# A hybrid decoder step on one core: who issues the cache pages, and a new table of places for the background work

## What is computed

```python
def mla_sample_attention(q_nope, q_rope, c_kv, k_rope, lat_past, kr_past, w_uk, w_uv):
    q_lat = jnp.einsum('bthd,chd->bthc', q_nope, w_uk)
    s_past = (jnp.einsum('bthc,bkc->bhtk', q_lat, lat_past)
              + jnp.einsum('bthr,bkr->bhtk', q_rope, kr_past)).astype(jnp.float32) * scale
    ...
    p = jax.nn.softmax(jnp.concatenate([s_past, s_new], axis=-1), axis=-1).astype(c_kv.dtype)
    o_lat = (jnp.einsum('bhtk,bkc->bthc', p[..., :P], lat_past) + ...)

# lat_past, kr_past: cache_kv_latent[l][page_table], cache_k_rope[l][page_table]:
# 8 sequences x 16 pages of 128 rows, 256 and 32 floats wide

merged = (g0 * (pool_y @ w_pool_out) + g1 * (mla_o @ w_mla_out) + g2 * (mem_o @ w_x_out)) @ w_o
h = x + merged

def peer_ffn(h):            # on rmsnorm(h), for each of 544 tokens
    q = jnp.einsum('nd,dhc->nhc', hf, lp['w_peer_q'])          # "queries"
    s1, s2 = q[..., :128] @ k1.T, q[..., 128:] @ k2.T           # 8 heads
    # top 16 of each, top 16 of their 256 sums: 128 experts a token, of 16384
    a = gelu(einsum('cd,ckd->ck', hc, peer_u[ic]))              # rows u
    return einsum('ck,ckd->cd', gate * a, peer_v[ic])           # rows v
```

## Time and profile before

| | |
|---|---|
| median of 3 runs | 2424.64 us (2421.26 to 2428.17) |
| the profiled execution | 2408.34 us |
| its span, first to last instruction | 2406.4 us |
| busy: PE, DVE, POOL, ACT | 1354.6, 1135.9, 1034.5, 299.8 us |
| moved by DMA | 688.00 MB, 570.49 MB of it by POOL's gathers |
| first gather, first GELU, second GELU | 533.8 us, 878.7 us, 1397.3 us |

### The profile page before, as it was taken

How to read it: one execution, slowest core, us unless ns; L and a number is a source line. 1 busy time by engine, 2 the same in 40 slices (tenths; PEclk the granted TensorE clock), 3 DMA queues, 4 the chain that set the end, 5 groups by cost and what they waited for, 6 DMA issues and landing times.

```text
span 2406.4 us, 22075 instructions
## 1 busy us (share of the span) xinstructions
PE 1354.6 (56%) x7122; PEld 811.6 (34%) x7122; DVE 1135.9 (47%) x2797; ACT 299.8 (12%) x758; POOL 1034.5 (43%) x1098
## 2 busy tenths in 40 slices
PE   7998999995444537898763865510035510035513
PEld 5874788783223324555541621100001100001100
DVE  2104521136757733344598156068967068850060
ACT  2214520022222121001010110000000000000000
POOL 0000000004233524565466146666666676666674
PEclk9998999996677658999876876655567655567656
DMA  6212035548697869999999669999999999999997
GB/s 198 74 59 59 1 105 152 149 128 307 224 309 245 325 249 325 373 374 350 364 386 399 215 235 354 374 391 376 374 352 357 364 391 382 371 353 366 376 382 270
DMA packets 337097, 688.00 MB, mean 286 GB/s; under 512 B 45319, under 2 KB 189608, under 8 KB 336975
## 3 DMA queue, kind: packets, MB, share of 16 engines
q0 software_dynamic: 156672, 570.49, 62.6%
q1 hardware_dynamic: 180311, 116.10, 16.6%
HBM read 682.36 MB, written 4.18 MB: 285 GB/s over the span
## 4 chain that ended last, share of the span: by engine, by line
PE 30%; DVE 22%; issue 12%; DMA 10%; another core or an unknown queue 9%; SPq 7%; POOL 5%; DVEq 3%; ACT 2%; POOLq 0%; ACTq 0%
PE bank L663 23%; DVE arena L1850 15%; POOL arena L629 5%; DMA arena<-in_w_x_out_dram 4%; DVEq L1786 3%; PE bank L659 2%; PE bank L1142 2%; SPq L510 2%; DMA arena<-in_cache_mem_v_dram 2%; SPq L507 2%; DMA arena<-in_peer_v_dram,arena 2%; SPq L504 2%; DMA arena<-in_w_mla_out_dram 1%; SPq L539 1%
## 5 line engine op out<-in xcount | busy, mean ns | idle before, releaser
L629 POOL DMA_INDIRECT arena<-in_peer_u_dram,arena x544 | 512.3, 942 | 926.1 <-DVE arena L1834 531.8
L663 PE MATMUL bank<-arena 128*128 128x256 f32 (+7 forms) x2940 | 714.9, 400 | 93.0 <-issue 48.1
L629 POOL DMA_INDIRECT arena<-in_peer_v_dram,arena x544 | 517.3, 951 | 426.7 <-PE bank L1142 193.0
L1850 DVE CUSTOM_DVE_ANT_0 arena<-arena,bank 128x1024 f32<-128x1024 f32 x544 | 638.1, 1216 | 43.8 <-issue 38.9
L663 PEld LDWEIGHTS bank<-arena 128*128 128x128 f32 (+2 forms) x2940 | 545.4, 194 | 263.2 <-issue 99.8
L1142 PE MATMUL bank<-arena 128*32 128x512 f32 x2176 | 377.8, 829 | 319.7 <-DMA arena<-in_peer_v_dram,arena 239.9
L659 PE MATMUL bank<-arena 128*128 128x128 f32 (+5 forms) x774 | 152.8, 349 | 586.4 <-issue 203.2
L659 PEld LDWEIGHTS bank<-arena 128*128 128x128 f32 (+5 forms) x774 | 117.2, 179 | 634.6 <-issue 246.5
L1142 PEld LDWEIGHTS bank<-arena 128*32 128x32 f32 x2176 | 80.7, 133 | 592.9 <-issue 591.5
L1178 ACT ACTIVATE arena<-bank 128x256 f32<-128x256 f32 (+12 forms) x399 | 156.6, 428 | 510.9 <-PE bank L663 150.4
L1879 DVE TENSOR_TENSOR arena<-arena,bank 128x1024 f32<-128x1024 f32 x5 | 6.1, 1220 | 361.6 <-PE bank L1142 194.3
(11 more groups left out here) (140 smaller groups left out, 722.3 us busy)
## 6 DMA issues: line engine op xcount, KB each, us to landing
arena<-in_w_in_dram SPq DMA_DIRECT2D x48, 512.0 KB
arena<-in_w_peer_q_dram SPq DMA_DIRECT2D x32, 512.0 KB
arena<-in_cache_kv_latent_dram SPq DMA_DIRECT2D x128, 128.0 KB
arena<-in_peer_u_dram,arena POOLq DMA_INDIRECT x544
arena<-in_peer_v_dram,arena POOLq DMA_INDIRECT x544
arena<-in_w_o_dram SPq DMA_DIRECT2D x8, 1024.0 KB, 7.8
arena<-in_w_in_dram SPq DMA_DIRECT2D x6, 1024.0 KB
arena<-in_w_pool_out_dram SPq DMA_DIRECT2D x16, 256.0 KB
```

Source lines behind the costliest of these rows:

```text
L629: pool.indirect_dma_start(out=ring[s % RING], out_offset=None, in_=table[0], in_offset=IndirectOffsetOnAxis(ap=ix, axis=0)).then_inc(land[ ...
L663: last = pe.matmul(dst, lhs(k), rhs(k), start=(k == 0), stop=(k == n - 1))
L1850: dve.tensor_tensor_reduce(ring[s % RING], ring[s % RING], h_dot, 1.0, 0.0, ALU.mult, ALU.add, act_a[:, p % 2, k:k + 1]).then_inc(u_free, 1)
```

## The change

It does two things. ACT gets three of the eight pages of each step from the third step on: `own_pages(s)` names the pages of SP (five) and of ACT (three, each with a table read of its own). ACT issues those of step s + 2 at the end of its third unit of step s. And the numbers in `background_ticks` are new.

```diff
+def own_pages(s):
+
+    mine = [(j, k) for j in range(4) for k in range(PGRP)]
+    return (mine, []) if s < 2 else (mine[0:5], mine[5:])
+
 def background_ticks():
 
     u0, u1 = PLACE["u", 0, 0], PLACE["u", 1, 0]
-    ticks = [u0 + 3 + 23 * i // 12 for i in range(3 * (STEPS + 1))]
...
-    ticks += [u0 + 109 + 7 * i // 4 for i in range(2 * (NB + 2))]
-    ticks += [u0 + 147 + 27 * h // 10 for h in range(2 * MERGE)]
...
-    ticks += [u1 + 74 + 3 * j for j in range(QJ + 2)]
+    ticks = [u0 + 3 + 5 * i // 3 for i in range(3 * (STEPS + 1))]
...
+    ticks += [u0 + 96 + 2 * i for i in range(2 * (NB + 2))]
+    ticks += [u0 + 138 + 13 * h // 5 for h in range(2 * MERGE)]
...
+    ticks += [u1 + 52 + 3 * j for j in range(QJ + 2)]
     return ticks
@@ load_pages on SP
                 for j in range(4):
                     n = (4 * a + j) * PAGES + g * PGRP
-                    _, pages = nc.values_load_multi_w_load_instructions(pagetab[0:1, n:n + PGRP], engines=[mybir.EngineType.SP], min_val=0,
-                                           max_val=cache_lat.shape[1] - 1)
-                    for k, page in enumerate(pages):
+                    ks = [k for jj, k in own_pages(s)[0] if jj == j]
+                    if not ks:
+                        continue
+                    _, pages = nc.values_load_multi_w_load_instructions(
+                        pagetab[0:1, n:n + len(ks)], engines=[mybir.EngineType.SP], min_val=0,
+                        max_val=cache_lat.shape[1] - 1)
+                    for k, page in zip(ks, pages):
@@ on ACT
+            def load_pages(s):
+
+                i, a, g = s % 3, s // HALVES, s % HALVES
+                if s >= 3:
+                    act.wait_ge(pv_mm, s - 2)
+                for j, k in own_pages(s)[1]:
+                    n = (4 * a + j) * PAGES + g * PGRP + k
+                    page = act.value_load(pagetab[0:1, n:n + 1], min_val=0, max_val=cache_lat.shape[1] - 1)
+                    act.dma_start(lat[i][:, j, k],
+                                  cache_lat[0][DynSlice(page, 1)].rearrange("a p c -> (a p) c")).then_inc(
+                        ld_page[i], 16)
+                    act.dma_start(rop[i][:, k, ROPE * j:ROPE * (j + 1)],
+                                  cache_kr[0][DynSlice(page, 1)].rearrange("a p c -> (a p) c")).then_inc(
+                        ld_page[i], 16)
@@ sample on ACT: ahead of the first step, and at the end of a step's third unit
+                act.wait_ge(ld_gain, 16 * 13)
...
+                    if s + 2 < STEPS:
+                        load_pages(s + 2)
```

More of the change, by code:

```diff
@@ L112 @@
 STEPS = 2 * HALVES
+def own_pages(s):
+    mine = [(j, k) for j in range(4) for k in range(PGRP)]
+    return (mine, []) if s < 2 else (mine[0:5], mine[5:])
 def background_ticks():
     u0, u1 = PLACE["u", 0, 0], PLACE["u", 1, 0]
-    ticks = [u0 + 3 + 23 * i // 12 for i in range(3 * (STEPS + 1))]
-    ticks += [u0 + 102 + 2 * i for i in range(3)]
-    ticks += [u0 + 109 + 7 * i // 4 for i in range(2 * (NB + 2))]
-    ticks += [u0 + 147 + 27 * h // 10 for h in range(2 * MERGE)]
-    ticks += [u1 + 22 + 27 * r // 10 for r in range(12)]
-    ticks += [u1 + 56 + 2 * t for t in range(3)]
-    ticks += [u1 + 64 + 3 * t for t in range(3)]
-    ticks += [u1 + 74 + 3 * j for j in range(QJ + 2)]
+    ticks = [u0 + 3 + 5 * i // 3 for i in range(3 * (STEPS + 1))]
+    ticks += [u0 + 90 + 2 * i for i in range(3)]
+    ticks += [u0 + 96 + 2 * i for i in range(2 * (NB + 2))]
+    ticks += [u0 + 138 + 13 * h // 5 for h in range(2 * MERGE)]
+    ticks += [u1 + 11 + 2 * r for r in range(12)]
+    ticks += [u1 + 37 + 2 * t for t in range(3)]
+    ticks += [u1 + 44 + 5 * t // 2 for t in range(3)]
+    ticks += [u1 + 52 + 3 * j for j in range(QJ + 2)]
     return ticks
```

## The result

The change takes 2411.05 us (median of 5 runs, 2405.87 to 2412.52), the kernel before in the same comparison 2426.28 us (2421.26 to 2432.35). The ratio is 0.9932, with an interval of 0.9912 to 0.9953: faster by some 16 us. Run once more beside others (`e11_change_again`) it is 0.9944 [0.9923, 0.9965]. The forecast was "about no change", 2426 us; the time lies in its range, but the change helps, which the forecast gave a chance of 0.35.

A forecast was written before the change was run, and what follows sets the result against it. Length is set by rows and background bytes passing before tile 1's GELU; only DMA rest can be won. Terms -10 + 3 + 12.5 - 4 = +1.5 us on 2424.64 gave 2426 us, range 2402 to 2450.

The forecast's parts named there:

- 13 steps, 13.1 to 12.3 us: Steps without DVE's picking: three pages on ACT shorten each from 13.1 to 12.3 us, -10 us (-30 to +13).
- two pick intervals: Two steps with DVE's picking of experts: ACT's 5.4 us of pages come on top, half shows, +3 us (0 to +11).
- rows fewer at the merge's start: New ticks: 9 rows fewer through when the merge begins, if the background takes the same time, 1.39 us each, +12.5 us.
- memory rounds and the way to the merge: Rounds of 11.5 us have room for four rows; later GELU of tile 0 mostly hidden by the ring: 0, up to +8.
- behind it: queries, stop: Queries start 31 us earlier, 1.2 of them cross POOL's stop ahead of tile 1's GELU, 3.2 us each: -4 us.
- The cost of a page: ACT's issue of one page, two DMAs and a table read: 1.56 to 2.07 us, three taken as 5.4 us.
- The rival that counted their window in full: Queries ahead of tile 1's GELU: 6 move at 4.85 us each, -20 instead of -4, 2410 us; chance 0.17.
- The slower rival: Steps: ACT's six DMAs each wait out one of SP's, 14.3 us a step, +27 in all, 2452 us; slower had chance 0.29.
- The carried 16 us: Whole kernel: the median's 16 us over the profiled 2408.34 us, carried over to the forecast, gathers taken to cost the same.

The follow-up runs named there:

- e11_change_again: The change once more, nothing altered, run beside other kernels: 0.9944 of the kernel before.
- e2_ticks_only: The change with all eight pages of every step on SP, only the ticks new: 0.9969 of the kernel before, 7.5 us less.
- e6_memory_13_later: The change with every tick behind the 16 steps 13 rows later, two rows to a memory unit: 0.9984 of the kernel before, 2422 us.
- e1_pages_only: The change with the ticks of before, so only the three pages on ACT are new: 0.9943 of the kernel before, 14 us less.
- e9_sparse: Two thirds of the queries behind the GELU of tile 1, seven rows to a step, six to a memory round, against the change: 0.9862 of before.
- e12_sparse_all_on_sp: The change with late queries, seven rows to a step and six to a memory round, and all pages back on SP: 0.9871 of the kernel before.
- e3_queries_back: The change with the queries' ticks 22 rows later, as before the change: 0.9917 of the kernel before.
- e7: The change with memory rounds from tick 90, all 20 memory units ahead of the GELU of tile 0, merge from 127: 0.9907 of before, 2404 us.
- e5_before_again: The kernel before once more, nothing changed, for a second profile: ratio 1.0012, profiled execution 2404.95 us.
- e4_queries_late: The change with twelve of the 18 query units put behind the GELU of tile 1: 0.9743 of the kernel before, 62 us less.

## Why the prediction was wrong

Between two chips of equal speed (the profiles of before and of `e11_change_again`) the sum reads, forecast and measured:

| term | forecast | measured |
|---|---|---|
| 13 steps, 13.1 to 12.3 us | -10 | 12.2 us: -11.8 |
| two pick intervals | +3 | -1.8 |
| rows fewer at the merge's start | 9 rows, +12.5 | 12 rows, +16.7 |
| memory rounds and the way to the merge | 0 | -9.9 |
| behind it: queries, stop | -4 | -1.5 |
| sum | +1.5 | -7.7 (with 0.6 for the first step's later start) |

**The step that failed** is the third term with its condition, "If the background took the same time". The rows were fewer, and each was paid for in the full stretch as the step says, but the background did not take the same time: the same 57 rows passed in 124.4 us instead of 134.3 (6.4 to 9.9 us less, over the two profiles of each kernel). The text took the rounds' 11.5 us as the rounds' own and saw room in them; it did not ask what POOL waited for there. The waits had it: 41.9 us for PE's weighing, because 11 of 20 units stood behind the GELU of tile 0, between v rows. The new table leaves six there. The prediction looked at this very edit (14 units ahead instead of 9) and counted only its price, 0 to +8, as a later GELU; it is the gain. `e2_ticks_only` shows that the ticks bring it without the pages, `e6_memory_13_later` that taking part of it away costs 10 to 12 us though 13 rows more are through. By the runs of single halves, the ticks were forecast at 12.5 - 4 = +8.5 us and measured at -7.5; the pages at -10 + 3 = -7, and measured at -14. (The terms were worked out for both parts together.) So the larger part of the miss, 16 us, is in the ticks; the 7 us of the pages are little more than an interval of 5 us to either side. The paragraph on what bounds the kernel had said that only rest counts; the term then counted rows.

**The steps** came out as worked in their length: 12.2 us for 12.3, SP nearly gone from the chain, the merge's start with rows missing. The cost of a page was at the lower end (1.6 us for 1.8). The mechanism was right that SP's issuing was the bound, and only half right on what follows: not ACT's chain alone, but ACT's and SP's parts at about the same length. And the 16 steps were named as one place of rest: three quarters of their rest is in the two picks, and the prediction's term of -10 us closed none of it. It was won only against what five rows to a step would have opened.

The Trainium skill ("DMA: Bandwidth & Descriptors", section "Issuing engines are not separate DMA queues") says of the issue time that a second issuer saves that it is usually small beside the DMA itself. Here `e1_pages_only` measured it at 14 us of 2426, and with seven rows to a step it is 2 us, not told from nothing (`e9_sparse` against `e12_sparse_all_on_sp`). So this case bears it out where the steps keep the DMA engines full (0.98 to 1.00), and not where one queue's issuing is the chain.

**The picks** had the wrong sign: DVE is busy for 26 of 29.7 us there before, and ACT's pages lie beside its work.

**The queries** went as forecast, one moved over the stop instead of 1.2, POOL's wait 59.5 us in the expected 55 to 62. The rival that counted their window in full is refuted for the change (`e3_queries_back`), but shows in the profiled execution of e7.

**The slower rival**, two issuers in each other's way, did not occur: ACT's DMAs mostly take 0.34 to 0.40 us beside SP's 0.33. A few take longer (one of 1.03 us at 604.16).

**The timed difference** is 13.5 to 16 us, the profiles' 7.7, or 4.4 with the second profile of before. The profiled executions themselves hold some of what lies between: before's in `e5_before_again` is 3 us under the median of its chip, the change's in `e11_change_again` 2.4 over its own (2401.06 for 2398.67). No place was found for it, so half of the measured gain is without a place in any trace.

**The carried 16 us** between profile and median were taken for the program's, "the gathers cost the same there as far as I can tell". They don't: on the chip where before has its median at 2427.51 us the 688 gathers take 1007 to 1009 us in the profiles, against 998. It cost the forecast nothing here, because before was timed at that level in the comparison too (2426.28 us).

## What to carry to other kernels

Where a shared resource sets the length, keep one ledger: the time in which it rests. Rows ahead or behind at some point are no gain or loss by themselves; ask at each edit which rest it opens or closes, and read from the waits of the engine that feeds the resource who closes it now. The largest rest is the first to ask about: moving two thirds of the queries past the GELU that all gathers waited for brought another 46 us, where the finer work on steps and rounds had brought 16. Of the rest that is left, the two picks have 37 us.

## What was unexpected of the hardware

PE comes to a crawl in one stretch: while u rows of tile 1 are gathered at the full DMA share, its matmuls start singly, 2.1 to 2.8 us apart, each 0.37 us long, and wait for nothing that the profile shows. In before:

```profile
1279.81 0.37 PE L1117 MATMUL bank<-arena 128*128 128x128 f32 x1 [2.43 <-issue]
1282.61 0.37 PE L1117 MATMUL bank<-arena 128*128 128x128 f32 x1 [2.43 <-issue]
1285.40 0.37 PE L1117 MATMUL bank<-arena 128*32 128x128 f32 x1 [2.43 <-issue]
```

This is what makes a query 24 to 43 us long there. Beside v rows, at a share of 0.88 to 1.02, `e4_queries_late` shows 8 to 19 us a query, and the quick execution of `e7_memory_ahead` 5 to 12 beside u rows at 1.04. So a full DMA share alone doesn't make the crawl. The clock granted to PE is near its lower level meanwhile (0.54 from 1270 to 1300 us in before), but a matmul is 0.37 us long even so, beside gaps of over 2. What PE waits for stays open; nothing here was tried on it.

One chip takes 1% longer than two others for gathers at the full share (1007 to 1009 us against 998 to 999 for the same 688), which is about as much as the change brings: spans of single profiles from different chips can't tell such a change.
